# A two-layer S5 and gated-attention block: each head's row of cumulative gates reaches the 128 partitions by a DMA from DRAM in place of a product of ones and a ScalarE copy

## The reference, cut to what matters

```
log_f = log_sigmoid(f_logit + b_f)                  # 512 tokens x 16 heads
cum   = cumsum(log_f, axis=tokens)                  # transposed to heads x tokens
s = einsum('bhqd,bhkd->bhqk', q_i, k) * scale
s = s + c_i[..., :, None] - cum[:, :, None, :]      # c_i: cum at the queries, cum: at the keys
s = where(kpos <= qpos, s, -1e30); p = softmax(s); o = p @ v
```

## Time and profile before

| | us |
|---|---|
| median of 3 runs | 3371.03 |
| lowest and highest | 3370.91, 3374.05 |
| span of the profiled execution, first to last instruction | 3371.7 |
| PE busy | 3219.6 (95%) |
| POOL busy | 1657.5 (49%) |
| DVE busy | 1408.6 (42%) |
| ACT busy | 1125.9 (33%) |

### The profile page before, as it was taken

How to read it: one execution, slowest core, us unless ns; L and a number is a source line. 1 busy time by engine, 2 the same in 40 slices (tenths; PEclk the granted TensorE clock), 3 DMA queues, 4 the chain that set the end, 5 groups by cost and what they waited for, 6 DMA issues and landing times.

```text
span 3371.7 us, 48606 instructions
## 1 busy us (share of the span) xinstructions
PE 3219.6 (95%) x18636; PEld 2504.3 (74%) x18636; DVE 1408.6 (42%) x2142; ACT 1125.9 (33%) x1508; POOL 1657.5 (49%) x1319
## 2 busy tenths in 40 slices
PE   5799998999999999999998989999999999999997
PEld 4688886878767877877877857777777777775576
DVE  8778783120153213223222054445445445345512
ACT  4354543233333223223233243233233233233421
POOL 2466662444557776776763434344344344443142
PEclk9899998999999999999999999999999999998999
DMA  3455556232212222222222232222222222223332
GB/s 134 139 164 171 171 169 172 100 138 88 99 52 86 87 83 79 87 79 83 87 77 73 100 120 90 83 97 72 84 89 80 80 85 84 76 83 114 106 133 87
DMA packets 124628, 343.72 MB, mean 102 GB/s; under 512 B 59600, under 2 KB 62672, under 8 KB 93904
## 3 DMA queue, kind: packets, MB, share of 16 engines
q1 hardware_dynamic: 124496, 341.77, 30.7%
HBM read 302.14 MB, written 34.87 MB: 100 GB/s over the span
## 4 chain that ended last, share of the span: by engine, by line
PE 79%; issue 7%; DVE 7%; POOL 4%; ACT 2%; DMA 0%; ACTq 0%; SPq 0%; POOLq 0%; DVEq 0%
PE bank L183 22%; PE bank L185 21%; PE bank L184 21%; POOL wlo L167 4%; PE bank L1391 3%; PE bank L1703 1%; PE bank L1048 1%; PE bank L1066 1%; PE bank L451 1%; PE bank L450 1%; DVE g L808 1%; ACT whi L162 1%; PE bank L1704 1%; PE bank L462 1%; PE bank L1778 1%
## 5 line engine op out<-in xcount | busy, mean ns | idle before, releaser
L167 POOL TENSOR_TENSOR wlo<-wraw,whi 128x512 fp32r<-128x512 f32 (+1 forms) x916 | 1244.7, 1389 | 1430.3 <-ACT whi L162 1430.3
L183 PE MATMUL bank<-rhi,whi 128*128 128x512 f32 x3648 | 1496.4, 410 | 87.1 <-DVE rlo L678 28.6
L185 PE MATMUL bank<-rhi,wlo 128*128 128x512 f32 x3648 | 1434.4, 393 | 0.0
L184 PE MATMUL bank<-rlo,whi 128*128 128x512 f32 x3648 | 1434.3, 393 | 0.0
L183 PEld LDWEIGHTS bank<-rhi,whi 128*128 128x128 f32 x3648 | 692.7, 190 | 305.9 <-issue 88.8
L185 PEld LDWEIGHTS bank<-rhi,wlo 128*128 128x128 f32 x3648 | 692.4, 190 | 149.2
L184 PEld LDWEIGHTS bank<-rlo,whi 128*128 128x128 f32 x3648 | 693.8, 190 | 141.1 <-issue 11.5
L162 ACT ACTIVATE whi<-wraw 128x2048 fp32r<-128x2048 f32 (+2 forms) x232 | 437.8, 1887 | 634.4 <-PE bank L185 495.1
L878 POOL TENSOR_TENSOR wraw<-wraw,vec 128x512 f32<-128x512 f32 x260 | 267.5, 1059 | 0.0
L790 DVE TENSOR_TENSOR ssum<-ssum,wk 128x512 f32<-128x512 f32 x30 | 21.6, 719 | 315.3 <-ACT wk L780 315.3
L780 ACT ACTIVATE wk<-bank 128x512 f32<-128x512 f32 x32 | 27.9, 872 | 240.1 <-PE bank L185 240.1
(11 more groups left out here) (363 smaller groups left out, 3241.3 us busy)
## 6 DMA issues: line engine op xcount, KB each, us to landing
wraw<-in_wall_dram SPq DMA_DIRECT2D x224, 1024.0 KB, 4.8
g<-in_bmat_dram SPq DMA_DIRECT2D x16, 512.0 KB, 5.6
g<-scr_e SPq DMA_DIRECT2D x128, 64.0 KB, 4.9
scr_a<-ssum SPq DMA_DIRECT2D x24, 256.0 KB, 2.1
g<-in_xp_dram SPq DMA_DIRECT2D x4, 1024.0 KB, 11.9
g<-in_cmat_dram SPq DMA_DIRECT2D x16, 256.0 KB, 4.7
scr_u<-wk SPq DMA_DIRECT2D x16, 256.0 KB, 5.9
scr_y<-wk SPq DMA_DIRECT2D x16, 256.0 KB, 2.2
```

Source lines behind the costliest of these rows:

```text
L167: ins = pool.tensor_tensor(wlo[:, slot, c], wraw[:, slot, c], whi[:, slot, c].bitcast(F32), ALU.subtract)
L183: pe.matmul(acc[slot][:, :], whk, rhi[:, k, :], start=(k == first), stop=False)
L184: pe.matmul(acc[slot][:, :], whk, rlo[:, k, :], start=False, stop=False)
L185: ins = pe.matmul(acc[slot][:, :], wlk, rhi[:, k, :], start=False, stop=(k == last))
```

## The change

The row of head h is now read from DRAM. SP writes `cum` once to a DRAM scratch `scr_c` (16 x 512) when the gates are ready, waits until it has landed, and then issues for each head one DMA that reads the row of 2 KB and writes it to all 128 partitions of `nb` (256 KB). In SP's stream this DMA stands behind the second of the head's four weight loads. It waits for `f_mx` of the head before, after which `nb` may be overwritten. DVE waits for the DMA's 16 counts of `f_nb` before `softmax_max`, and subtracts the row, as it is no longer negated. Gone are the masking on DVE (L944), the product on PE (L1033), the copy on ACT (L1005), and the waits `f_cm`, `f_b`, `fg_cc` of these.

```
-            d.wait_ge(f_nb, h + 1)
+            d.wait_ge(f_nb, 16 * h + 16)
...
-                                             mf["nb"][:, 0:n], ALU.add, ALU.add)
+                                             mf["nb"][:, 0:n], ALU.add, ALU.subtract)
...
-            wait(d, f_b, h)
-            d.tensor_scalar(cmask, cum, ident[0:SC, h:h + 1] if isinstance(h, int) else
-                            ident[0:SC, bass.ds(h, 1)], -1.0, ALU.mult, ALU.mult).then_inc(f_cm, 1)
...
-            act.wait_ge(f_b, h + 1)
-            if prev:
-                act.wait_ge(f_mx, h)
-            act.activation(mf["nb"], ps_st[:, :], ACT.Copy).then_inc(f_nb, 1)
...
+        def fox_sp(sp, h):
+
+            for i in range(4):
+                w_load_next(sp, 4 * h + (N_FOX + 2 + i), (i + 1) % 2)
+                if i == 1:
+                    if isinstance(h, int) and h == 0:
+                        sp.wait_ge(fg_c, 1)
+                        sp.dma_start(scr_c, cum).then_inc(fc_wr, 16)
+                        sp.wait_ge(fc_wr, 16)
+                    else:
+                        sp.wait_ge(f_mx, h)
+                    row = scr_c[h:h + 1, :] if isinstance(h, int) else scr_c[bass.ds(h, 1), :]
+                    sp.dma_start(mf["nb"], row.to_broadcast([P, T])).then_inc(f_nb, 16)
...
-            pe.wait_ge(f_cm, h + 1)
-            if isinstance(h, int) and h == 0:
-                pe.wait_ge(fg_cc, 1)
-            wait(pe, f_nb, h)
-            pe.matmul(ps_st[:, :], ones[32:32 + SC, :], cmask, start=True, stop=True).then_inc(f_b, 1)
...
-            tile_pairs(sp, 50, 144, sp_weights)
+            tile_pairs(sp, 50, 64, sp_weights)
+            w_load_next(sp, 66, 0)
+            fox_sp(sp, 0)
+            with sp.Fori(1, KT) as h:
+                fox_sp(sp, h)
+            w_load_next(sp, 131, 1)
+            tile_pairs(sp, 130, 144, sp_weights)
```

More of the change, by code:

```diff
@@ L844, in program @@
         cum = ssum[0:SC, :]
-        cmask = ssum[32:32 + SC, :]
+        scr_c = nc.dram_tensor("scr_c", [SC, T], F32).ap()
         mask = wk[:, 6272:6400]
@@ L852, in program @@
         fg_cc = sem("fg_cc")
-        f_cm = sem("f_cm")
-        f_b = sem("f_b")
+        fc_wr = sem("fc_wr")
         f_nb = sem("f_nb")
```

## The result

The changed kernel takes 3384.15 us (median of 8 runs, 3377.58 to 3386.27), the kernel before 3371.99 (8 runs, 3369.30 to 3374.05). The ratio is 1.0031, 95% interval 1.0022 to 1.0040: slower by 0.3%. The forecast was 3349.3, with a range up to 3357, so the sign is wrong as well as the size. The profiled execution of the changed kernel has a span of 3375.8 us at a mean clock of 0.973 (before: 3371.7, 0.976).

The account below looks back on a forecast made before the run. The prediction took PE, busy 760.47 of 761.00 us in the heads, as the bound. It summed 3371.0 - 19.2 (heads 1 to 15) - 0.95 - 1.54 (head 0) = 3349.3 us, range 3347 to 3357.

Parts of the forecast that it names:

- The heads: PE, heads 1 to 15: the product leaves, 1.28 us saved a head, 19.2 us in all, low end 15.8.
- Head 0: PE in head 0: project n + 2 starts 0.95 us earlier, and a clock drop costing 1.54 us goes.
- The clock drop: PE's drop behind head 0's product was to go, saving 1.54 us; rival that it stays: 3350.8 us, chance 0.17.
- The prediction's 1.2 GHz: PE's lower clock level, said to hold for nearly all of 3.52 us in head 0; the upper is 2.4 GHz.
- ACT, DVE, SP: Copies and masks dropped from ACT and DVE gain nothing, head 0 aside; SP's added DMA in each head costs 0.
- the bounds of 2.1 and 4.9: Landing time in us of SP's DMA spreading a 2 KB row over 128 partitions; 4.9 was taken.
- the 4.2 to 9.8: Head 0: us for two landings, write and row, with 8.1 us until the next weight load; no cost even at the upper end.
- Outside the heads nothing is touched: Stages behind the heads: unchanged, only starting 21.7 us earlier.
- 2 us each way: Allowance for clock drops elsewhere that need not fall where they fell before.
- given back: Rival: an unseen input makes PE wait; 3360 us if half is lost, 3371 if all; chance 0.07, of which 0.03 no change.
- Slower: Rival: the spreading DMA holds SP's queue, deciding from T = 26 us, 15 us per microsecond beyond; chance 0.03.
- the slacks of one turn: SP's queue in the heads: 11.4 us covering the load, 6.9 its landing, 7.9 the reader, giving the 26 us limit.

Follow-up runs that it names:

- the run with two transposes: Changed kernel with two identity transposes (4 places) added on PE ahead of the RWKV loop: 3352.13 us.
- the two other versions: Changed kernel with a hint that the RWKV loop's jump back is taken, 3351.31 us, and with two transposes added ahead of the loop, 3352.13 us.
- the 240 places: Kernel before with 120 identity transposes added on PE between the heads and the RWKV loop: 3404.63 us, ratio 1.0095.
- at 254: Kernel before with the head of PE's RWKV loop at place 254 of a block of 256 instructions: 3405.85 us, ratio 1.0096.
- at 248: Kernel before with the head of PE's RWKV loop at place 248 of a block of 256 instructions: 3409.52 us.
- at 0, 56 or 64: RWKV loop's head at that place of a 256 block: 0 in the changed kernel, 3349.42 us; 56 and 64 in the kernel before, 3372.28 and 3371.76.

## Why the prediction was wrong, point by point

**The heads: right.** 15 x 1.28 = 19.2 was forecast, 19.3 measured. The third matmul ends 0.70 us after the transposes (forecast 0.69, by the earlier trace rows). PE is busy for all 761.00 us of the stretch and never waits for wlo.

**Head 0: right.** From the end of the small transposes to the ninth matmul's start: 987.62 to 993.10 before, 985.23 to 988.17 after, 5.48 against 2.94 us. That is 2.54 saved, where 0.95 + 1.54 = 2.49 was forecast. The project starts 1.02 us after the transposes, behind L943. The clock drop went, and none of the seven traces of the changed kernel and its versions shows it there, while all seven of the old kernel's do (some 3.4 us at 0.50 near 990). So this step held, though I had only one row for it. No view has the clock in GHz. What the traces show in its place is how far one 128 x 512 matmul of a project starts behind another: 0.427 us at 0.50 (990.18 to 992.74 before, six steps), that is 512 / 427 = 1.2 columns a ns, and 0.227 us at 1.00 (1726.57 to 1732.93 after, 28 steps), 2.26 a ns. The prediction's 1.2 GHz matches the first if a column is a cycle, an estimate; its 2.4 is the double of that, and no time rests on either.

**ACT, DVE, SP: right.** The spreading row lands in 3.3 us:

```profile
wk<-scr_c SPq DMA_DIRECT2D x15, 256.0 KB, 3.3
```

It lies between the bounds of 2.1 and 4.9; I took 4.9, too much, at no cost. SP waits 2.6 us for f_mx (2.7 forecast), and in the last head the load behind goes out at 1722.45, 11.4 us after f_mx at 1711.1 (11.4 forecast). In head 0 the write is issued at 975.92, the row at 977.53, and the next load at 983.87, on time. DVE never waits for the row, only for PE's L1049. The write landed in 1.6 us. With a row's 3.3 that makes 4.9, inside the 4.2 to 9.8 that the prediction took for the pair and under the 8.1 at hand.

**"Outside the heads nothing is touched": this step failed.** It was true of the work and not of the code. Taking 16 instructions out of PE's stream moved all that follows, and the RWKV loop's head came to lie at most four instructions ahead of the end of a 16 KB block (four places more clear the end, as the run with two transposes showed). Each of six returns cost 4.7 us in the mean: 28.0, more than the 21.8 gained (19.3 and 2.5; the 24.2 us of lead hold another 2.4 that are no effect of the change, see below). The allowance beside that step, "2 us each way", was for clock drops; there was none for code. With the loop moved away from that place the kernel takes 3349.3 and 3349.4 us, the forecast number, and 3351.3 and 3352.1 in the two other versions: 20.5 to 23.0 us under the old kernel's runs of the same round, where 21.7 was forecast. So the sum of the terms was complete but for this one, which none of the rivals had. That two versions meet the forecast to a tenth is luck: the runs of one kernel differ by 2 us and more, and the old kernel's median is 3371.0 in one set and 3372.0 in the next. The rival "given back" is nearest in kind, but it ends at 3371, 13 us short of the measured time, and it has PE wait for an input in the heads, which no row shows. "Slower" had a chance of 0.03, and for a reason, SP's queue, that plays no part here.

**The rest, partly open.** 3349.3 + 28.0 = 3377.3 is the profiled execution (3377.58), which is also the fastest of the eight; the median is 6.6 above it. The three versions of the old kernel with the same stalls lose more behind the loop as well. From the last L1274 to the end of the span are 361.4 us with the 240 places, 361.2 at 254 and 359.1 at 248, but 353.8 before. So the 2 us that I allowed for clock drops elsewhere were too few once stages had moved. A stretch of 25 us there, first with the 240 places, then before, has the lower clock throughout and only in part:

```profile
3098.00:3123.00 25.00, 23.52 (x60) 13.28 (x60) 9.28 (x26) 11.57 (x34) 9.03 (x8) 0.50 0.22 60
```

```profile
3073.00:3098.00 25.00, 23.63 (x83) 12.98 (x81) 12.13 (x34) 12.56 (x37) 9.02 (x8) 0.68 0.22 63
```

In the profiled execution of the changed kernel this part is short (3021.2 to 3375.8, 354.6 us). That its other executions lose some 7 us there is likely by this, but no trace of one shows it. The 2.4 us by which the changed kernel was ahead already when it reached head 0 (984.82 against 987.20) are no effect of the change either: the old kernel with the 240 places, which is the same up to there, reaches that point at 984.95.

## What to carry to other kernels

An edit on the engine that bounds the kernel moves all of its later code. Where a long loop follows, read the waits on "issue" ahead of the first instruction of its body and the packet count of the instruction queue, before and after. If a change gives less than its stage shows, place the loop's head on a block's start before believing in contention; here that was worth 35 us. In a forecast, leave room for it: the range should hold (number of returns) x (one fetch and a clock drop) on the slow side, here 6 x 4.7 = 28 us. And a slack that a loop uses in each turn is found from the cycle of the queue, not by adding up the slacks of one turn.

## What the hardware showed that I had not expected

- A return to a loop head 2 to 8 instructions ahead of a 16 KB block's end showed two fetches in series, about 3 us apart (2305.1 and 2308.1 in the changed kernel, 2333.6 and 2336.8 at 248), and cost 4.1 to 5.0 us in the mean (24.8 to 29.8 us over six returns), the clock's part included; 16 instructions ahead of it 0.8 us, and at 0, 56 or 64 nothing. One fetch at the return was hidden in the kernel before: it began some 3 us ahead of the body's first product (2327.0 and 2330.11), and PE shows no gap there.
- One packet more for each pass on the instruction queue cost nothing where it wasn't in series (3372.3 and 3371.8 us at places 56 and 64, 3372 before).
- PE's granted clock fell to 0.50 behind some stands and not behind others, and the length of the stand alone doesn't decide it: in the changed kernel it fell after 2.23, 2.47, 2.80 and 3.15 us and not after 2.57 and 3.08; with the head at 248 it fell after five stands of 1.6 to 1.9 us.
